# Decode attention of a hybrid layer: page numbers fetched together, places in the buffer dealt anew, scores of two sequences in turns

## The reference, cut to what matters

```python
# NB = 8 sequences, DL = 8 new tokens each, 16 pages of 128 tokens, G = 2 key heads, R = 4 queries a key head, D = 64
past = gather_pages(cache_nsa_slc_kv, page_table)          # page_table: (8, 16) numbers into a pool of 160 pages
s_c = einsum('blgrd,bngd->blgrn', q, k_c) * D**-0.5 - slopes * dist_c     # k_c: 32 compressed blocks of 64 tokens
p_c = masked_softmax(s_c);  o_cmp = p_c @ v_c
imp = sum_r p_c;  idx = top_k(imp with the own block forced, 16)          # blocks that each query may look at
o_slc = attention over the tokens of the blocks in idx, with ALiBi distances
o_win = banded attention over the last 512 tokens
o = g0 * o_cmp + g1 * o_slc + g2 * o_win
```

## Time and profile before

| | us |
|---|---|
| median of 3 runs | 3144.06 |
| lowest, highest | 3140.66, 3151.16 |
| profiled execution | 3156.4 |
| its span | 3154.6 |
| PE busy in the span | 3011.9 |
| decode stage on PE in it | 855.95 to 1000.9 |

### The profile page before, as it was taken

One profiled execution on the slowest core, in us unless ns is written; L12 is line 12 of the kernel. 1 busy time (PEld: TensorE's weight loads), 2 busy tenths in 40 slices (PEclk: granted clock), 3 DMA queues, 4 the chain that ended last, 5 costly groups with the idle time before them and its releaser, 6 DMA issues.

```text
span 3154.6 us, 44020 instructions
## 1 busy us (share of the span) xinstructions
PE 3011.9 (95%) x18571; PEld 2704.7 (86%) x18571; DVE 1031.7 (33%) x2179; ACT 629.9 (20%) x1207; POOL 661.1 (21%) x354
## 2 busy tenths in 40 slices
PE   7999999999978999999999998998999999999998
PEld 5766767667636999999999998977999999999998
DVE  2102224676535242222222233166242122222224
ACT  3002111366533220000000013044220000000004
POOL 1020000011101223223222221202232223222320
PEclk9999998999988999999999999978999999999999
DMA  5634320220142111111111111100111111111111
GB/s 149 201 87 121 125 62 11 65 58 6 45 127 97 48 47 41 41 54 41 41 43 52 41 41 48 46 1 14 27 41 41 41 54 41 41 41 53 41 41 71
DMA packets 209624, 180.22 MB, mean 57 GB/s; under 512 B 36746, under 2 KB 190400, under 8 KB 208835
## 3 DMA queue, kind: packets, MB, share of 16 engines
q1 hardware_dynamic: 202416, 149.32, 16.0%
q0 software_dynamic: 6848, 28.04, 3.0%
q10 hardware_dynamic: 162, 0.04, 0.0%
HBM read 162.97 MB, written 19.51 MB: 58 GB/s over the span
## 4 chain that ended last, share of the span: by engine, by line
PE 87%; DVE 7%; SPq 2%; issue 2%; ACT 2%; DMA 0%; DVEq 0%; ACTq 0%
PE ps L1997 53%; PE ps L586 8%; PE ps L711 4%; PE ps L2013 3%; PE ps L582 3%; PE ps L1382 2%; PE ps L2384 2%; PE ps L1395 2%; PE ps L1418 2%; SPq L979 1%; PE ps L2368 1%; SPq L977 1%; PE ps L2247 1%; PE ps L2351 1%; DVE arena L2090 1%
## 5 line engine op out<-in xcount | busy, mean ns | idle before, releaser
L1997 PE MATMUL ps<-spot,w_hi 128*128 128x368 f32 (+1 forms) x6732 | 1303.7, 328 | 15.1 <-DVE spot L2213 12.1
L1997 PEld LDWEIGHTS ps<-spot,w_hi 128*128 128x128 f32 x6732 | 1138.4, 188 | 19.3 <-DVE spot L2213 15.3
L1997 PE MATMUL ps<-spot,w_lo 128*128 128x368 f32 x3420 | 751.8, 328 | 0.0
L1997 PEld LDWEIGHTS ps<-spot,w_lo 128*128 128x128 f32 x3420 | 589.7, 188 | 0.0
L1974 POOL CAST w_hi<-arena 128x2048 fp32r<-128x2048 f32 x79 | 152.9, 1936 | 1421.2 <-DMA arena<-in_w_gate_up 774.3
L1975 POOL TENSOR_TENSOR w_lo<-arena,w_hi 128x2048 fp32r<-128x2048 f32 x79 | 367.8, 4655 | 6.3
L2106 DVE TENSOR_TENSOR arena<-arena,ps 128x368 f32<-128x368 f32 (+1 forms) x312 | 147.4, 528 | 479.9 <-PE ps L1997 453.2
L586 PE MATMUL ps<-arena 128*128 128x368 f32 (+1 forms) x768 | 246.4, 479 | 1.5 <-DVE arena L1210 1.5
L2188 ACT ACTIVATE arena<-arena 128x1088 f32<-128x1088 f32 x44 | 49.0, 1114 | 893.3 <-DVEq L2204 893.3
L586 PEld LDWEIGHTS ps<-arena 128*128 128x128 f32 x768 | 147.6, 195 | 88.8 <-issue 7.3
L2208 DVE TENSOR_TENSOR arena<-arena,ps 128x368 f32<-128x368 f32 x132 | 62.4, 528 | 446.3 <-PE ps L1997 441.1
(11 more groups left out here) (444 smaller groups left out, 2885.1 us busy)
## 6 DMA issues: line engine op xcount, KB each, us to landing
arena<-in_w_gate_up SPq DMA_DIRECT2D x88, 512.0 KB, 4.3
arena<-in_w_down SPq DMA_DIRECT2D x22, 1024.0 KB, 4.9
arena<-in_cache_nsa_cmp_kv SPq DMA_DIRECT2D x128, 128.0 KB, 2.1
arena<-in_cache_nsa_slc_kv SPq DMA_DIRECT2D x128, 128.0 KB, 2.5
arena<-in_w_in_even SPq DMA_DIRECT2D x9, 1024.0 KB, 6.5
x_spill<-arena POOLq DMA_DIRECT2D x1, 4352.0 KB, 14.7
arena<-in_x_prompt SPq DMA_DIRECT2D x8, 512.0 KB, 6.9
arena<-in_cmp_w_k POOLq DMA_DIRECT2D x16, 256.0 KB, 4.5
```

The source lines that it names most:

```text
L1997: mm = nc.tensor.matmul(ps[:, 3 * s + j, 0:b - a], w, x[:, a:b], start=m == 0, stop=m == len(order) - 1)
```

## The change

- **Page numbers.** `page_numbers` fetches the 16 numbers of a sequence with one load, and `dec_sp` calls it before the wait that the sequence's pages have. Pages 3 now wait for the last unit but one of the prompt's attention, not for its end, and stand ahead of the constants `dec_late`, which are issued after pages 4.
- **Places.** Sequences 6 and 7 get other halves: 6 waits for the keys of sequences 2 and 3, 7 for the values of the first pair. POOL's window load of 7 waits for the same.
- **Order on PE.** A chunk is transposed for both sequences of a pair, then scored for both (`score_pair`): 256 columns of the even sequence, 256 of the odd one, and again. The first chunk of pair 2 and of pair 3 is transposed inside `values`.
- **DVE** reads the first pair's scores chunk by chunk between the steps of the ranking; one table of it is handled in two halves. The gating of `zT` is moved between pairs, and one small addition a pair is new.
- **ACT** splits the exponential of `ds` in two and deals the pieces between the copies of keys. The logarithm and exponential of `rs_flat` stand behind the first pair's probabilities.

```diff
-        KEYS_AT = ((0, 0), (1, 0), (2, 0), (3, 0), (4, 0), (0, 0), (4, 0), (0, 0))
-        VALS_AT = ((0, 1), (1, 1), (2, 1), (3, 1), (4, 1), (1, 0), (2, 0), (1, 1))
+        KEYS_AT = ((0, 0), (1, 0), (2, 0), (3, 0), (4, 0), (0, 0), (3, 0), (1, 1))
+        VALS_AT = ((0, 1), (1, 1), (2, 1), (3, 1), (4, 1), (1, 0), (2, 0), (0, 1))
...
+            pages = page_numbers(sp, 3)
+            sp.wait_ge(sem("at_pv"), len(UNITS) - 1)
+            dec_pages(sp, 3, pages)
+            pages = page_numbers(sp, 4)
             sp.wait_ge(sem("z_total"), 1)
-            sp.wait_ge(sem("at_oT"), 1)
+            dec_pages(sp, 4, pages)
             load(sp, "dec_late")
-            for b in range(3, NB):
-                if b >= 5:
-                    turned(sp, {5: 1, 6: 4, 7: 5}[b])
-                dec_pages(sp, b)
+            pages = page_numbers(sp, 5)
+            turned(sp, 1)
+            dec_pages(sp, 5, pages)
+            pages = page_numbers(sp, 6)
+            turned(sp, 3)
+            dec_pages(sp, 6, pages)
+            pages = page_numbers(sp, 7)
+            sp.wait_ge(sem("dt_pv"), 1)
+            dec_pages(sp, 7, pages)
...
+        def page_numbers(sp, b):
+            _, pages = nc.values_load_multi_w_load_instructions(table[0:1, b * NPAGE:(b + 1) * NPAGE], [mybir.EngineType.SP],
+                                                                min_val=0, max_val=159)
+            return pages
...
+            def score_pair(p, j):
+                pair = [(b, slice(b % 2 * HD, (b % 2 + 1) * HD)) for b in (2 * p, 2 * p + 1)]
+                group_copied(pe, dgroups.index(("k", 2 * p + 1, j)))
+                for h in range(2):
+                    for b, part in pair:
+                        mm = nc.tensor.matmul(ps[part, j, h * 256:(h + 1) * 256], qbd[:, b],
+                                              kt[b % 2][:, 4 * j + 2 * h:4 * j + 2 * h + 2].rearrange("p a b -> p (a b)"),
+                                              start=True, stop=True)
...
+                if bp + 2 < NPAIR:
+                    turn_pair(bp + 2, 0)
...
+            turn_pair(0, 0)
+            for p in range(NPAIR):
                 for j in range(5):
...
+                    if j < 4:
+                        turn_pair(p, j + 1)
+                    elif p == 0:
+                        turn_pair(1, 0)
...
+                    if p == 1 and j in (0, 4):
+                        pe.wait_ge(sem("dt_read"), 1 + j // 4)
...
+                    score_pair(p, j)
...
+                    if p == 1 and j == 1:
+                        pe.wait_ge(sem("dt_dve"), 4)
...
+            for p in range(2, NPAIR):
+                copy_keys(act, p, 0)
+                copy_keys(act, p, 1)
+                exp_selected(p - 1, 0)
+                copy_keys(act, p, 2)
+                exp_selected(p - 1, 1)
+                copy_keys(act, p, 3)
+                exp_window(p - 1)
+                copy_keys(act, p, 4)
...
+            read_chunk(0)
+            read_chunk(1)
             loaded(dve, "dec_late")
...
+            ties(0)
+            read_chunk(2)
+            read_chunk(3)
+            dve.wait_ge(sem("dt_qk"), 5)
+            v.tensor_tensor(dw[:, 0:WIN0], ps[:, 4], dec_win, ALU.add).then_inc(sem("dt_read"), 1)
+            ties(1)
```

More of the change, by code:

```diff
@@ L1663, in dec_sp @@
             sp.wait_ge(sem("ssm_fin_stored"), 16)
-            dec_pages(sp, 0)
-            dec_pages(sp, 1)
+            for b in range(2):
+                dec_pages(sp, b, page_numbers(sp, b))
             sp.wait_ge(sem("kt_s"), 1)
@@ L1787, in dec_pe @@
                         pe.wait_ge(sem("dt_dve"), 1)
[L1788 removed]
+                    if p == 0 and j == 2:
                         pe.wait_ge(sem("z_read"), 1)
[L1790 removed]
+                    if p == 0 and j == 4:
                         pe.wait_ge(sem("dt_dve"), 3)
[L1792 to L1798 removed]
@@ new lines, in dec_pe @@
+                    if p >= 2 and j == 0:
+                        pe.wait_ge(sem("dt_read"), 2 * p)
+                    if p >= 2 and j == 4:
+                        pe.wait_ge(sem("dt_ob"), p - 1)
+                    score_pair(p, j)
+                    if p == 0 and j == 1:
+                        pe.wait_ge(sem("dt_dve"), 2)
+                        for bp in range(NPAIR):
+                            mm = nc.tensor.matmul(ps[:, 5, 256:256 + NCB], pair_sum[:, 96 - 32 * bp:224 - 32 * bp], pc[:, bp],
+                                                  start=bp == 0, stop=bp == NPAIR - 1)
+                        mm.then_inc(sem("dt_c"), 1)
@@ L1807, in dec_pe @@
+                    if p == 1 and j == 1:
+                        pe.wait_ge(sem("dt_dve"), 4)
+                        nc.tensor.matmul(ps[:, 5, 384:512], pair_back, sel_bd.rearrange("p b n -> p (b n)"), start=True, stop=True)\
+                            .then_inc(sem("dt_c"), 1)
+                if p >= 2:
+                    turn_out(p - 2)
+                if p:
+                    values(p - 1)
             turn_out(2)
@@ L1837, in dec_act, with exp_selected, exp_window @@
         def dec_act(act, E):
-            copy_keys(act, 0)
+            DS_PART = ((0, 16), (16, NCB + 1))
+            def exp_selected(bp, k):
+                a, b = DS_PART[k]
+                if k == 0:
+                    act.wait_ge(sem("dt_m"), 2 * bp + 1)
+                nc.scalar.activation(ds[:, a:b], ds[:, a:b], ACT.Exp, scale=-1.0, bias=small[:, 0:1],
+                                     accum_out=small[:, 2 + 4 * k:3 + 4 * k])
+            def exp_window(bp):
+                act.wait_ge(sem("dt_m"), 2 * bp + 2)
+                nc.scalar.activation(dw, dw, ACT.Exp, bias=small[:, 1:2], accum_out=small[:, 3:4])\
+                    .then_inc(sem("dt_e"), 1)
+            copy_keys(act, 0, 0)
             act.wait_ge(sem("dt_dve"), 1)
             nc.scalar.activation(pc, pc, ACT.Exp).then_inc(sem("dt_ce"), 1)
-            copy_keys(act, 1)
-            copy_keys(act, 2)
+            for j in range(1, 5):
+                copy_keys(act, 0, j)
+            copy_keys(act, 1, 0)
+            for j in range(1, 5):
+                copy_keys(act, 1, j)
+            exp_selected(0, 0)
+            exp_selected(0, 1)
+            exp_window(0)
+            copy_probs(act, nc.scalar.copy, "act", 0)
             act.wait_ge(sem("z_read"), 1)
```

155 lines of the change are left out of this document (69 added, 86 removed).

## The result

| | before | after |
|---|---|---|
| median, runs side by side | 3146.91 (6 runs) | 3120.98 (6 runs) |
| lowest, highest | 3140.66, 3155.78 | 3117.01, 3126.61 |
| profiled execution, its span | 3156.4, 3154.6 | 3121.67, 3119.9 |
| decode stage on PE (first transposition of keys to last of an output) | 145.0 | 117.3 |

The ratio is 0.9917, with a 95% interval of 0.9897 to 0.9936: the change makes the kernel 25.9 us faster, and 3121.0 lies within 3103 to 3128, 9.2 above the 3111.8 of the forecast. The two spans differ by 34.7. Of that the stage gives 27.7 (853.80 to 971.11 now, 855.95 to 1000.9 before); 2.2 lie ahead of it and 4.9 behind it.

A forecast was written before the change was run, and what follows sets the result against it. SP's issue of page numbers and DMAs was taken to bound the decode stage. Fewer page waits and cheaper scores, less a new table wait, made it 32.3 us shorter: 3144.06 - 32.3 = 3111.8, range 3103 to 3121, widened to 3128.

The forecast's parts named there:

- numbers of 16: SP's fetch of a sequence's 16 page numbers by one load: 3.0 us, between bounds of 1.2 and 4.9.
- tables issued: SP issues `dec_late` behind pages 4, at 869.2 on the profiled clock; landing at 874, range 873 to 877.
- pair 1's first score: PE waits 7.3 us on DVE, held by the late table, and goes on at 878.1 with 1.6 of low clock.
- pair 2 ends: PE's four chunks, one score and small ones, 8.6 + 1.0 + 0.2, and 0.4 for ACT: at 913.2.
- rival B: PE's score halves don't overlap, a chunk stays at 3.18: 20.8 us less, 3123.3; chance 0.08.
- SP idle before pages 5, 6 or 7: Sign expected in SP's queue: SP stands idle ahead of these page loads.
- Scores: Four scores of a pair's chunk on PE, alternating between partition halves: 1.0 instead of 2.02, a chunk 2.15 instead of 3.18.
- 0.4 for ACT: Allowance in pair 2 on PE for banks that wait on a piece of ACT's exponential: 0.4 us.
- E: PE starts over at each switch between halves, a chunk costs 4.96: 11.5 us slower, 3155.6; chance 0.03.
- Rival C: ACT becomes the bound, exponential pieces keep banks from PE in pairs 2 and 3: 25.9 us less, 3118.2; chance 0.11.
- Rival D: SP's page numbers come no faster, 9.0 for 16: 13.6 us less, 3130.5; chance 0.04.
- The tail: Stage end through DVE's masks, ACT's exponential, POOL's weight split and the last values: 22.5 us, stays.

The follow-up runs named there:

- e3_no_turns: Changed kernel with both score matmuls of the even sequence first, then both of the odd one, instead of in turns; 3122.44 us, ratio 0.9912.
- e9_whole: Changed kernel with two score matmuls of 512 columns a chunk in place of four of 256; 3121.74 us, one run.
- e10_before_halves: Kernel before with each score of 512 columns split into two of 256, same order otherwise; 3149.15 us, one run.
- e2_numbers_singly: Changed kernel with the 16 page numbers of a sequence fetched one by one again, at the same places; 3140.97 us, ratio 0.9969.
- after_again: The changed kernel itself, unedited, run again beside the best variants on one chip; 3125.89 us, ratio 0.9929.
- e6_hoisted_tables: Changed kernel with numbers of sequences 3 and 4 fetched before the wait for the prompt's attention, tables before pages 4; 3125.67 us, ratio 0.9928.
- e7_pool_later: Changed kernel with POOL's first split of the dense weights waiting for DVE's last copy of pair 3's probabilities; 3114.79 us, ratio 0.9882.

## Why the prediction was right, point by point

Times from the start of the stage, the prediction's (from 855.95) and the trace's (from 853.80):

| step | predicted | measured | the step's own miss |
|---|---|---|---|
| numbers of 16 | 3.0 (1.2 to 4.9) | 5.2 | +2.2 each |
| tables issued | 13.25 | 17.1 | +3.9 |
| pair 0 scored and turned | 14.85 | 13.7 | -1.2, hidden |
| pair 1's first score | 22.15 | 25.97 | +3.8 |
| probabilities of pair 0 | 34.35 | 38.8 | +0.6 |
| first values end | 47.05 | 50.2 | -1.3 |
| pair 2 ends | 57.25 | 59.5 | -0.9 |
| second values end | 69.15 | 75.4 | +4.0 |
| pair 3 ends | 79.35 | 86.4 | +0.8 |
| third values end | 90.15 | 97.2 | 0.0 |
| stage ends | 112.65 | 117.3 | -2.4 |

- **Direction, mechanism and size** held: waits for pages nearly gone, one new wait ahead of pair 1 for a table, and a stage 27.7 shorter where 32.3 were forecast.
- **The 9.2 between forecast and median** have three parts: 4.6 by which the sum missed the stage; 2.9 because the kernel before has a median of 3146.91 over six runs, not the 3144.06 of the first three; 1.7 between the stage's gain (27.65) and the medians' (25.93). By its own terms the forecast's range is 3102.7 to 3124.2 (9.1 down, 12.4 up), not 3103 to 3121, and rival B's 893.3 adds up to 893.9; neither changes the reading.
- **The mis-sized term is the fetch of numbers**: 5.2 measured, 3.0 taken, and my highest bound of 4.9 was also too low. That bound was built as one load of 0.27 and sixteen times the rest of a number's time. The register part came out below it, 0.25 and not 0.29; what I had not thought of is that a load of sixteen takes 0.98 and not 0.27. I had taken the middle of two bounds with a reason (0.147 may only be waiting for the load) that the rows refute: it is 147 ns here too, with the load long done.
- **It reaches the path at two places.** Numbers 4 stand ahead of the tables: with 2.2 for them, a DMA issue stretched to 1.15 and pages 3 ending 0.9 later, the tables are 3.9 late, and so is pair 1's first score. Numbers 5, 6 and 7 add 6.6 to SP's queue, so that pages 7 are out 69.0 after the start of the stage (922.8) and not 58.8: the wait of 2.44, which I had put at none, and 1.4 of low clock behind it make the +4.0, and 0.8 more falls on pair 3. "SP idle before pages 5, 6 or 7" was wrong for the same cause.
- **Scores** were right in size (1.02 for 1.0; the chunk 2.04 for 2.15, which with the 0.4 for ACT that did not come gives the -0.9 of pair 2) and wrong in their reason. I took the values' row as the nearest and read its turns as the cause; e3_no_turns, e9_whole and e10_before_halves show that neighbourhood is.
- **Rivals B and E** are out by the chunk's 2.04. The Trainium skill's rule for E ("TensorE: Matmul & The Clock Gate", Part 3, The mechanism: a weight load overlaps running matmuls only where the row group differs) does not hold for these two halves, which differ in columns alone: two scores with their weight loads last as long as one (1.01), and their first records start within 0.01 of each other in e9_whole.
- **Rival C**: PE waited 0.2 for ACT's copies. ACT's two copies take 1.07 of 2.04, so that the limit that the Trainium skill's page "TensorEngine Tiling (Array Packing)", section PSUM Bottleneck, warns of was near but not met.
- **Rival D** is out, and e2_numbers_singly is its kernel. It was worked out at 13.6 less; the ratio of 0.9969 is 9.8 less, and so is the stage. The wait for pages came near (13.3 for 12.2); the one for the tables was 16.4, some 3.6 more than worked out.
- **The tail** is 2.4 shorter, and I had left it as it was. That is luck of the profiled execution: before, its values took 6.22, part of them at the low clock, and after, 3.71; in after_again they took 5.31, and the stage ends at 118.6, 5.9 behind the forecast and not 4.6. What PE waits for there did change with the kernel: POOL's first conversion no longer doubles DVE's 128x1088 operation (3.04, then 1.34), while the 128x2 one grew from 3.31 to 4.35. A tail in which two engines meet is not a constant.

## What to carry to other kernels

Where a queue issues without a gap, sum up everything that it issues until the last thing that somebody waits for: moving one issue forward moves another back, and only what leaves the busy stretch (numbers fetched ahead of the first wait, fewer instructions a number) shortens it. Put matmuls of 64 stationary columns next to one that writes the other 64 output partitions; cutting or alternating them adds nothing. And before calling a tail unchanged, look for two operations of DVE and POOL that end at the same hundredth, and see whether rows that both profiles share ran at the same clock.

## What the runs showed of the hardware that was not expected

- A load of one number into a register of SP took 0.27, one of sixteen 0.976 (L1698); each number's register instructions then take 0.25 (857.57 to 861.09 in after, fourteen steps), of which one instruction is 147 ns, whether the load is recent or not.
- Issuing a DMA costs SP 0.52 with full rows (861.50 to 862.02 above) and 0.73 in two pieces, and now and then one takes 1.15 (867.16).
- Two matmuls of 512 columns and 64 stationary columns into the two halves of the output partitions last 1.01 together (e9_whole), as one does between transpositions; five in a row into one half take 0.89 each (before).
- A table of 256 KB that lands 4.1 after its issue needs 10.7 when the DMA share is 1.04 (e6_hoisted_tables).
- DVE's operation on 128x2 took 4.35 beside POOL's on 128x2048 (after) and 0.16 without it (e7_pool_later).
- The same 64 matmuls of the same kernel took 3.71 in one execution and 5.31 in another, at granted clocks of 1.00 and 0.68 (after, after_again).
